# Gate/up weights of a mixture of experts loaded in two halves of the inner dimension, with one wait for each half

## What is computed

```python
# hier_moe: 4 groups of 8 experts, each token takes its best group and the 2 best experts in it
for gi in range(N_GROUPS):
    a = jnp.einsum('btd,edf->btef', h, w_e_gate[gi])      # D_MODEL 1024 -> D_EXPERT 256
    u = jnp.einsum('btd,edf->btef', h, w_e_up[gi])
    act = jax.nn.silu(a) * u * combine[..., gi, :, None]
    out = out + jnp.einsum('btef,efd->btd', act, w_e_down[gi])
```

## Time and profile before

| | |
|---|---|
| median of 3 runs | 1196.32 us (1195.31 to 1197.29) |
| the profiled execution | 1194.61 us, its span 1192.8 us |
| TensorE (PE) busy | 1071.5 us, 90% of the span |
| VectorE (DVE) busy | 560.3 us, 47% |
| ScalarE (ACT) busy | 249.6 us, 21% |
| GpSimd (POOL) busy | 153.2 us, 13% |
| moved by DMA | 226.33 MB, 190 GB/s over the span |
| mean granted clock of TensorE | 0.959 of full speed |

### The profile page before, as it was taken

One profiled execution on the slowest core, in us unless ns is written; L12 is line 12 of the kernel. 1 busy time (PEld: TensorE's weight loads), 2 busy tenths in 40 slices (PEclk: granted clock), 3 DMA queues, 4 the chain that ended last, 5 costly groups with the idle time before them and its releaser, 6 DMA issues. The chain is left out here.

```text
span 1192.8 us, 14860 instructions
## 1 busy us (share of the span) xinstructions
PE 1071.5 (90%) x5798; PEld 704.7 (59%) x5798; DVE 560.3 (47%) x1105; ACT 249.6 (21%) x671; POOL 153.2 (13%) x299
## 2 busy tenths in 40 slices
PE   4699998999999999999989999999945998978776
PEld 2254777777777887889667777754423333322222
DVE  2222737567888494476655555353365111110127
ACT  2100010467632122464110010101110110100012
POOL 2000500111414000023010000100011211111101
PEclk9899999999999999899989999999967999998898
DMA  9967743142424444124362423359276999999984
GB/s 363 287 226 194 221 76 74 25 126 73 74 62 71 106 71 80 37 73 129 120 238 71 75 90 118 88 158 318 95 254 225 415 421 415 419 419 419 420 301 145
DMA packets 93089, 226.33 MB, mean 190 GB/s; under 512 B 21278, under 2 KB 39951, under 8 KB 78782
## 3 DMA queue, kind: packets, MB, share of 16 engines
q1 hardware_dynamic: 83270, 202.70, 52.0%
q10 hardware_dynamic: 4624, 12.75, 3.1%
q0 software_dynamic: 5120, 9.88, 2.4%
HBM read 210.60 MB, written 23.08 MB: 196 GB/s over the span
## 5 line engine op out<-in xcount | busy, mean ns | idle before, releaser
L2473 PE MATMUL ps<-w_gate_up,xT 128*64 128x512 f32 x528 | 130.1, 632 | 21.3 <-DMA w_gate_up<-w_e_up 21.3
L2473 PEld LDWEIGHTS ps<-w_gate_up,xT 128*64 128x64 f32 x528 | 40.6, 145 | 108.1 <-issue 78.8
L2635 DVE TENSOR_TENSOR act<-silu_gate,ps 128x256 f32<-128x256 f32 x17 | 7.2, 421 | 200.5 <-ACT silu_gate L2430 200.5
L659 PE MATMUL ps<-hT,w_ring 128*128 128x288 f32 x384 | 96.6, 412 | 3.6 <-PEq L106 3.6
L659 PEld LDWEIGHTS ps<-hT,w_ring 128*128 128x128 f32 x384 | 73.3, 193 | 23.6 <-issue 3.9
L2490 PE MATMUL ps<-w_down,actT 128*64 128x512 f32 x264 | 62.1, 599 | 8.8 <-DVE actT L2639 8.8
L1308 PE MATMUL ps<-hT,w_ring 128*128 128x288 f32 x264 | 67.8, 407 | 0.0
L1593 DVE SCALAR_TENSOR_TENSOR conv_y<-z_staged,convT,conv_y 128x600 f32<-128x600 f32 x72 | 59.7, 842 | 8.4 <-ACT conv_y L1047 6.6
L422 PE MATMUL ps<-w_ring,hT 128*128 128x512 f32 x128 | 57.6, 610 | 6.1 <-DMA w_ring<-w_in 6.1
L1308 PEld LDWEIGHTS ps<-hT,w_ring 128*128 128x128 f32 x264 | 49.4, 190 | 13.1 <-issue 0.5
L422 PEld LDWEIGHTS ps<-w_ring,hT 128*128 128x128 f32 x128 | 24.7, 196 | 36.4 <-issue 30.1
(11 more groups left out here) (538 smaller groups left out, 1980.2 us busy)
## 6 DMA issues: line engine op xcount, KB each, us to landing
w_ring<-w_in SPq DMA_DIRECT2D x16, 2048.0 KB, 13.9
w_gate_up<-w_e_gate SPq DMA_DIRECT2D x32, 1024.0 KB
w_gate_up<-w_e_up SPq DMA_DIRECT2D x32, 1024.0 KB
w_down<-w_e_down SPq DMA_DIRECT2D x32, 1024.0 KB, 25.7
w_ada_slots<-w_ada SPq DMA_DIRECT2D x10, 2048.0 KB, 9.1
w_ring<-w_ada SPq DMA_DIRECT2D x2, 2048.0 KB, 12.1
w_ring<-w_pa SPq DMA_DIRECT2D x2, 2048.0 KB, 7.8
w_ring<-w_pb SPq DMA_DIRECT2D x2, 2048.0 KB, 8.1
```

What stands on the lines that cost most here:

```text
L659: last = nc.tensor.matmul(psum[:, bank + hf, 0:HALF], w[:, c, 128 * q:128 * q + 128], x[:, c, HALF * hf:HALF * hf + HALF], start=c == 0, s ...
L2473: last = te.matmul(psum[side(u), s % 2, :], xT[:, s % 2, c, side(u)], gu[s % GU_BUFS][:, u, :, c, :], start=c == 0, stop=c == KC - 1)
```

## The change

A step's gate/up loads are issued in two halves of the inner dimension: first the rows c = 0 to 3 of gate and up of both experts, then the rows c = 4 to 7. A step of two experts then has eight loads of 512 KB (pieces of 4 KB) where it had four of 1 MB; the lone step has eight of 256 KB (pieces of 2 KB) where it had four of 512 KB. The second half raises a semaphore of its own, `gu_late`. TensorE waits for the first half ahead of its matmuls as before (the four loads of it give the same count of 64), and for the second half ahead of c = 4. Bytes, buffers and matmuls are the same, and so are the down loads.

```diff
             for c in range(KC):
+                if c == KC // 2:
+                    pe.wait_ge(m.gu_late[s % GU_BUFS], 64 * (s // GU_BUFS + 1))
                 for u in range(1 if s == LONE_AT else 2):
...
     parts = 2 // len(experts)
-    for u, e in enumerate(experts):
-        for k, name in enumerate(("w_e_gate", "w_e_up")):
-            w = ins[name][0].rearrange("g e (p c) f -> (g e) p c f", p=128)
-            for h in range(parts):
-                cs = slice(KC // parts * h, KC // parts * (h + 1))
-                sp.dma_start(m.gu[s % GU_BUFS][:, u, k, cs], w[e][:, cs]).then_inc(m.gu_loaded[s % GU_BUFS], 16)
+    for h in range(2):
+        for u, e in enumerate(experts):
+            for k, name in enumerate(("w_e_gate", "w_e_up")):
+                w = ins[name][0].rearrange("g e (p c) f -> (g e) p c f", p=128)
+                for part in range(parts):
+                    n = KC // 2 // parts
+                    cs = slice(KC // 2 * h + n * part, KC // 2 * h + n * (part + 1))
+                    sp.dma_start(m.gu[s % GU_BUFS][:, u, k, cs], w[e][:, cs]).then_inc((m.gu_late if h else m.gu_loaded)[s % GU_BUFS], 16)
...
             m.gu_loaded = [kept(f"gu_loaded{i}") for i in range(GU_BUFS)]
+            m.gu_late = [kept(f"gu_late{i}") for i in range(GU_BUFS)]
```

## The result

The changed kernel takes 1201.39 us (median of 5 runs, 1200.42 to 1204.63) where the kernel before takes 1196.32 us (5 runs, 1195.31 to 1199.03). The ratio is 1.0043, 95% interval 1.0026 to 1.0059: slower by about 5 us. The forecast was 1194.5 us, 1.8 us faster, so it is on the wrong side, and outside its range.

What follows compares the result with a forecast made beforehand. The prediction took weight transfers at 418 GB/s to bound the expert stage. Its terms, -3.44 + 0.6 + 0.3 + 0.7 = -1.8 us, took the median from 1196.3 to 1194.5 us, range 1192.4 to 1198.8.

Steps and rivals of the forecast that it cites:

- The price of smaller pieces: Expert-stage gate/up loads: completions 0.6, 4 KB pieces 0.3, lone step's 2 KB pieces 0.7; together 1.6 us later landing.
- the rows: Profile windows 1001-1012 and 1014-1024 us: 4 KB piece 0.156 us, 8 KB 0.311 us, so half within 0.2%.
- The second reading: Gate/up 7 to 10, partly in halves: 41.33 us against 41.45 at the six steps' pace, so no price shows.
- Two waits in place of one: TensorE, last gate/up step: first half done when the last load lands, 3.65 us remain instead of 7.09; 3.44 us gained.
- The closing clock: Closing matmuls may lose their low-clock stretch (5.08 us for 8 against 3.44): 1.6 us more gain, 1192.9 us; chance 0.06.
- SyncE's eight issues: Eight gate/up issues a step instead of four: queue holds about 7 MB or 17 us, far from empty; costed at nothing.
- the signs of being wrong: Rate under 405 GB/s from 924 to 1134 us, landing past 1150, low clock after 1145, or closing-load wait at 1155.
- Small pieces are free: Gate/up loads: tiny packets overlap others, lone step's 2 KB pieces are hidden; whole 3.4 us stay, 1192.9 us; chance 0.28.
- On the line to 2 KB: Gate/up transfers, 920 to 1145 us: 4 KB pieces 5% over half, price 8.1 us less 3.4, 1201.0 us; chance 0.11.
- A fixed cost per load: Gate/up queue: each of 56 more loads costs 0.13 us, 7.5 us in all, 1201.1 us; chance 0.04.
- halves not in order: DMA engines interleave loads, first half completes just before the last; nothing gained, pieces cost 1.6 us, 1197.9 us; chance 0.05.
- The closing loads become the bound: Pairs' loads behind the expert stage come too late for TensorE: gain falls by 1 to 2 us, 1196 us; chance 0.06.

Runs made afterwards that it cites:

- x10: Kernel before with eight 512 KB gate/up loads a step, each a quarter of one matrix of both experts in 2 KB pieces, one wait; 1215.5 us, ratio 1.0142.
- x2: Changed kernel with four 1 MB gate/up loads a step, each half of one matrix of both experts, 4 KB pieces, two waits; 1202.0 us, ratio 1.0035.
- x1: Changed kernel with its eight loads in 4 KB pieces, but TensorE waits for both halves ahead of its first matmul; 1211.1 us, ratio 1.0096.
- x4: Kernel before with the change's halves (4 KB pieces) and two waits in steps 15 and 16 alone; 1199.4 us, ratio 1.0007.
- x5: Kernel before, four loads in 8 KB pieces, gate loads ahead of up, TensorE waiting for each matrix; 1195.7 us, ratio 0.9986.
- x6: Kernel before with gate loads ahead of up in all steps (8 KB pieces), two waits in steps 15 and 16 only; 1196.5 us, ratio 0.9996.
- x12: Kernel before with two 2 MB loads a step, gate then up, 8 KB pieces, a wait for each; 1196.3 us, ratio 0.9986.
- x14: x12 with the eight gate rows and the norm row issued behind the pairs' loads, on their own semaphore; 1193.7 us, ratio 0.9962.
- x9: Changed kernel with the lone step alone loaded as before (four whole loads, one wait); one execution, 1198.3 us.
- x15: Kernel before with only the gate rows and norm row issued behind the pairs' loads; 1196.3 us, ratio 0.9995.
- x13: Kernel before with two 2 MB gate/up loads a step instead of four of 1 MB, 8 KB pieces, one wait; one execution, 1193.6 us.
- x3: Kernel before with each 1 MB gate/up load cut in two by partitions (64 each), 8 KB pieces, one wait; 1360.7 us, ratio 1.133.

## Why the prediction was wrong

**The price of smaller pieces** is the step that failed. The mechanism was named, but its size was wrong. The forecast took a 4 KB piece to cost half an 8 KB one within 0.2%, and with completions and the lone step came to 1.6 us; 5.6 us were measured. With them the sum is -3.44 + 5.6 = +2.1 us. The spans differ by 5.7: the other 3.4 us are low clock (1.7 and 1.65 us), which the sum had at nothing, see below. The two stretches of 210 us hold enough packets to do the same sum properly. Each has 16 x 210 = 3360 us of engines. Before, 9372 pieces of 8 KB and 2673 under them; after, 3017 and 15,418, of which 1024 are the lone step's 2 KB pieces (taken at 0.090 us; 0.084 changes little); the rest are tiny at 0.0104 us. Both equations together give 0.309 us for 8 KB and 0.159 us for 4 KB: 2.9% over half. Two 4 KB pieces cost 2 x 0.159 - 0.309 = 0.009 us more than one of 8 KB, which is what x10 and x2 gave (9.4 and 9.3 ns). So the pieces took about 3.9 of the 5.6 us, an estimate, or 2.7 at the 6.5 ns of x1 and x10. How the other 1.7 us fall to the 52 further loads (x2 and the changed kernel differ by 1.0 us) and to the second wait or the order of loads (1.0 us between the groups of 8 KB) is not settled: x1, without the second wait, should land sooner than the changed kernel and lands 0.4 us later.

Why did the rows not show it? The windows of 10 and 11 us hold 36 and 77 packets for each engine, and a packet across the edge counts whole or not at all: one 8 KB piece for each of 16 engines is 5 of 160 us, 3%, which is the whole effect. The second reading compared 41.33 with 41.45 us, where 2.9% on 3.15 MB is 0.2 us, and steps differ among themselves by 0.6 us. The forecast said that this reading was too coarse to exclude a price on each load, and used it nevertheless against a price on each piece.

The rows had the right number in view: a tiny packet's 0.0104 us. The forecast charged it to completions alone. It is about what each further packet cost at 4 and 2 KB too, and 6,656 more pieces x 0.0104 / 16 = 4.3 us, with 0.6 us of completions 4.9 us, which alone would have put the forecast on the other side. The Trainium skill (DMA: Bandwidth & Descriptors, the note over the measured table under Bandwidth) puts the floor of a 4 KB transfer down to 64 packets of about 10.5 ns each, measured on GpSimd's queue. The runs come near it on SyncE's, 6.5 to 9.4 ns, and show that it is paid on pieces of 4 KB as well.

**Two waits in place of one** was right as far as it goes. The halves land in order, the first half is done before the second is there, and 3.65 to 3.67 us remain behind the landing at the full clock (x4, x5, x6, x12, x14). The waits were not those of the forecast: it had 2.0 and 1.6 us in step 16, and the trace has none and 2.26 us. In the profile of the changed kernel 1.7 us of the gain went to the low clock, which set in behind the last wait of 2.26 us. x9 has it too (5.35 us). That was one of the rivals, with a chance of 0.07.

**The closing clock** was on the list with the wrong sign. A first row of 5.08 us held a part at the low clock and was given a chance to lose it; it runs nearly all at the low clock instead, 6.73 us. In x9, x14, x12, x6 and x5 it is 6.2 to 6.7 us too. What decides it is open. The gap ahead of these matmuls alone is not it: 3.73 us in x15, which then takes 5.37, and 3.60 us in x14, which takes 6.71. Nor is it alone that gate/up 16 has only half of its work behind its last wait: x2 and x4 have that too and take 5.17 and 5.21 us, behind gaps of 4.20 and 5.99 us.

**SyncE's eight issues** left the DMA engines no less busy (1.02 in both), and the queue does hold far fewer bytes when the loads are smaller: the last load was issued at 1132.97 and landed 17.9 us later, where it was 30.4 us before.

Of the signs of being wrong that the forecast named, two came: a landing past 1150 us (1150.92) and a low clock after 1145. The rate, 409 GB/s, lies between its right and its wrong, and a wait on the closing loads is missing.

**The rivals.** *Small pieces are free* is out. *On the line to 2 KB* was the nearest, 1201.0 us for 1201.39, but by luck in part: it put 8.1 us on the pieces and nothing on the clock, where 5.6 and 3.4 us were found. *A fixed cost per load* of 0.13 us is out by x12 and x13, and by x2, which has 52 loads fewer than the changed kernel and lands 1.0 us sooner (0.02 us a load, about half of it the completions); *halves not in order* is out by the trace. *The closing loads become the bound* did not hold for the changed kernel, where TensorE finds the pairs there at 1172.14. It did hold for every other split version (waits of 1.9 to 3.1 us for the pairs in x2, x4, x5, x6 and x12) except x9 and x14. That the late landing spares the changed kernel was not shown: x2 lands 1.0 us sooner and waits 2.04 us.

## What to carry to other kernels

Where a stage is bound by transfers, count its packets before its loads: cutting a load along the contiguous run of each partition adds a packet's overhead for every further piece, cutting it between matrices adds none. A price of a few per cent can't be read off a window of 10 us; it has to come from a stretch of some hundred packets an engine, or from a packet's overhead times the packets added. And when the last wait of a stage is made shorter, look at what is queued for the stage behind it: here the gain showed only when nine rows copied to many partitions no longer stood ahead of the loads that were wanted next.

## What the runs showed of the hardware

- A gate/up stage in loads over 64 partitions ran at 258 GB/s where 128 partitions gave 418, with the DMA engines busy throughout (x3). With 4.19 MB of gate/up and 2.10 MB of down a step, and the latter at 418 GB/s, the halves alone come to about 217 GB/s (24.4 - 5.0 = 19.4 us for 4.19 MB), an estimate. The Trainium skill (SBUF — State Buffer, Door 1: The DMA port swizzle) gives about 218 GB/s for 64 partitions, and says in the section "Can I just issue two DMAs to hit both halves?" that two at once, one for each half, gave only 6% more than one. The estimate agrees with both.
- TensorE's low clock does not follow the length of one wait alone: in the changed kernel gate/up kept the full clock after 2.27 us of waiting (gate/up 12, at 1077.62) and ran at the low one after 2.26 us (gate/up 16); in x14 it ran low after 1.92 us (at 1132.15) and in x4 after 1.97 us. From 924 to 1134 us the changed kernel and x12, with two waits of up to 2.3 us a step, had a granted clock of 1.00; x2, also with two waits, had 0.97, and the kernel before, with one of up to 4.2 us, 0.95.
- The stall in the middle of the closing matmuls (3.65 us in x1, 3.84 in x10, 1.64 in x3, in no other kernel here) is not explained.
